# A four-layer transformer kernel on one core: another order of the modulation units in TensorE's stream

## The chip, the core and the metric

The kernel runs on one core of a Trainium2 chip. The core has five engines that run their own instruction streams and meet at semaphores: TensorE (PE, matrix products; its weight loads are listed as PEld), VectorE (DVE), ScalarE (ACT), GpSimd (POOL) and SyncE (SP). SP and ACT issue transfers between HBM and the on-chip memory SBUF; 16 DMA engines carry them. The metric is the device time of one execution in microseconds (us), lower is better. The time of before is the median of three runs.

## What is computed

Two blocks of two layers each work on 256 latent and 256 context tokens with 2048 features in float32. Each layer computes, from a condition vector, shift, scale and gate of its features (the modulation), normalizes and modulates x, projects it, runs attention (in layers 2 and 3 also a multi-scale pooling branch), gates the result to y, projects y and adds it to x by the gate. Cut to the first block:

```python
def first_block(x, c, ctx, c_ctx, w_ada, b_ada, norm_g, w_in, ..., w_out, final_g):
    sc, sc_ctx = jax.nn.silu(c), jax.nn.silu(c_ctx)
    for l in range(DEPTH):
        shift, scale, gate = jnp.split(sc @ w_ada[l] + b_ada[l], 3, axis=-1)
        shift_c, scale_c, gate_c = jnp.split(sc_ctx @ w_ada[l] + b_ada[l], 3, axis=-1)
        h_lat = rms_norm(x, norm_g[l]) * (1.0 + scale[:, None]) + shift[:, None]
        h_ctx = rms_norm(xc, norm_g[l]) * (1.0 + scale_c) + shift_c
        lat_a, lat_b = mixer_inputs(h_lat, w_in[l], ...)
        ctx_a, ctx_b = mixer_inputs(h_ctx, w_in[l], ...)
        o_a, o_b = block_attention(...), block_attention(...)
        x = x + gate[:, None] * merge_groups(o_a, lat_a[3], o_b, lat_b[3], w_out[l])
        ...
    return rms_norm(x, final_g)
```

The modulation `sc @ w_ada[l]` has 2048 x 6144 weights per layer, 48 MB, and depends on the condition alone, so it can be computed at any time before its layer needs it.

## The kernel before

**Slots.** The weights of all projections are 500 slots of 512 KB (`w_raw`, a ring of RAW = 4). Each slot is split into a high part by ACT (`high`, line 589, `w_high`) and a low part by DVE (`low`, line 911, `w_low`), rings of SPL = 2, and PE multiplies three products of high and low parts per block (line 1420, 24 per slot, 512 columns wide where all tokens take part, 256 where only the latent ones do). `low(n)` needs `high(n)`, `high(n)` needs PE to be through with slot n - 2, and SP issues slot n when PE is through with slot n - 4.

**Phases.** `plan_phases` lists them. A layer has: `root` (root of the mean square of x), `apply` (modulation of x into `h_high` and `h_low`, ACT line 647, DVE lines 984 and 1012, one of 16 chunks at a time), then linear phases in rounds of 8 slots k0 to k7: q, kv, cq, ckv, g_mla, kr, g_gqa, short phases and the attention `mla` in layers 0 and 1; q, k, v, pool_v, mix, pool_g, attn_g in layers 2 and 3. Then `ysplit` (ACT line 878 and DVE line 1408 split y from `mix_a` and `mix_b`, called Q and G, into `h_high` and `h_low`) and `out`, four rounds. Layers 0 and 2 work on all tokens, 1 and 3 in most phases on the latent ones. The phases cq to g_gqa (pool_v to pool_g) carry a first attention between their products. (i, k) below is slot k of round i. Round 0 of q and out runs in the order PAIRED, so that its first slots need only the first chunks.

**Units.** The modulation weights are 192 units of 1 MB; 16 of them are a span, the 2048 columns of one of shift, scale and gate of a layer. A unit is four products on PE (`span_unit`, line 1516; the profile counts 8 records). The first 36 run in the opening, from six places: four halves of Q and G, and the two halves of `ada_w`. The other 156 alternate between the two halves of `ada_w`. With `ada = n`, each of a phase's first n rounds has four: two behind slot k1 and two behind slot k5 (`ADA_AFTER = (1, 1, 5, 5)`). The end of a span is followed by a row copy on ACT, four small products on PE (`span_cols`, at k6) and four small adds on DVE (`span_columns`, at the round's end). A span's sum stands in the PSUM bank AD all the while; the attention `mla` uses that bank and B for its outputs in turn.

**SP's queue.** SP issues in the order of the phases, a unit behind the slot behind which it runs. A unit first waits until PE has used the last but one (`ada_used`), since its place is the same. Whatever is behind it in the program waits with it.

**The layer boundary.** After the last products of out, PE sums squares of x by columns (`token_sums`, line 1465), ACT and DVE make the inverse root, PE spreads it (`x_broadcast`, line 1473), DVE and ACT start with `apply`.

**ysplit.** All engines meet at its start (`handed_over`). ACT then issues the load of x from HBM into `x_residual` (lines 869, 872, 875), whose place the attention had used.

## Time and profile before

| | us |
|---|---|
| median of 3 runs | 3137.79 |
| lowest and highest | 3133.08, 3138.83 |
| profiled execution, its own time | 3129.61 |
| its span, first to last instruction | 3127.8 |
| PE busy | 2958.3 (95%) |
| DVE busy | 1587.0 (51%) |
| ACT busy | 1021.5 (33%) |
| mean granted clock of TensorE | 0.977 |

Busy times are those of the profiled execution. A timeline row gives start, length, engine, line, operation, what is written and read, and in brackets the idle time ahead of it with what ended it. "SPq" and "ACTq" are the instructions with which SP and ACT issue a transfer; the length is that of issuing. The granted clock is 1.00 at 2.4 GHz and 0.50 at 1.2 GHz.

### The profile page before, as it was taken

To read this page: it belongs to the slowest core of one execution; us is meant where nothing else is said; L and a number is where in the kernel's file an instruction comes from. 1 tells how busy PE (TensorE), PEld (TensorE's weight loads), DVE (VectorE), ACT (ScalarE), POOL (GpSimd) and SP (SyncE) were. 2 spreads that over 40 slices of the span, in tenths; PEclk is the share of its full clock that TensorE was granted. 3 is DMA by queue.
4 is the path that set the end of the run, shared out by engine and by line. 5 is a ranking of instruction groups with operands and counts; after the bars stand their busy time and mean duration, and the time that the engine had idled before them with its cause. 6 is when DMAs were issued, how large, how long until landed. Compare 5 with 4: busy or idle time off the path is not lost. (4 is left out here: it accounts for less than half of the span.)

```text
span 3127.8 us, 41128 instructions
## 1 busy us (share of the span) xinstructions
PE 2958.3 (95%) x17192; PEld 2372.8 (76%) x17192; DVE 1587.0 (51%) x2512; ACT 1021.5 (33%) x1510; POOL 102.0 (3%) x157
## 2 busy tenths in 40 slices
PE   6899999999998999998999999999989989999988
PEld 2577777776776878886777778767767778798888
DVE  4334434356336544455563553555563365738574
ACT  3222243225113233334332222334441132225453
POOL 0000000000000000000000000430000000004000
PEclk9999999999998999999989999999999989999999
DMA  9644343231544555624745344323455433232455
GB/s 406 267 172 154 126 148 128 88 108 72 186 174 173 204 192 189 221 96 153 279 164 192 129 179 160 136 105 131 155 185 188 172 103 114 93 102 90 146 169 169
DMA packets 129161, 501.94 MB, mean 160 GB/s; under 512 B 14160, under 2 KB 39504, under 8 KB 104144
## 3 DMA queue, kind: packets, MB, share of 16 engines
q1 hardware_dynamic: 109104, 474.96, 42.6%
q10 hardware_dynamic: 19872, 24.35, 2.3%
q8 instruction: 136, 2.23, 0.3%
q14 instruction: 49, 0.40, 0.0%
HBM read 484.05 MB, written 8.39 MB: 157 GB/s over the span
## 5 line engine op out<-in xcount | busy, mean ns | idle before, releaser
L1420 PE MATMUL products<-h_high,w_high 128*128 128x512 f32 (+1 forms) x3424 | 1254.8, 366 | 92.0 <-DVE h_low L1012 30.9
L1420 PE MATMUL products<-h_low,w_high 128*128 128x512 f32 (+1 forms) x3424 | 1194.3, 349 | 0.0
L1420 PE MATMUL products<-h_high,w_low 128*128 128x512 f32 (+1 forms) x3424 | 1193.7, 349 | 0.0
L911 DVE TENSOR_TENSOR w_low<-w_raw,w_high 128x1024 fp32r<-128x1024 f32 x500 | 614.0, 1229 | 807.1 <-ACT w_high L589 803.6
L589 ACT CAST w_high<-w_raw 128x1024 fp32r<-128x1024 f32 x500 | 523.1, 1046 | 1384.8 <-PE products L1420 1243.8
L1420 PEld LDWEIGHTS products<-h_high,w_high 128*128 128x128 f32 x3424 | 662.2, 193 | 298.8 <-issue 151.0
L1420 PEld LDWEIGHTS products<-h_high,w_low 128*128 128x128 f32 x3424 | 662.4, 193 | 81.4
L1420 PEld LDWEIGHTS products<-h_low,w_high 128*128 128x128 f32 x3424 | 664.1, 194 | 78.3 <-issue 10.1
L1420 PE MATMUL products<-w_high,h_high 128*128 128x256 f32 x640 | 183.7, 287 | 5.4 <-DVE w_low L911 4.9
L1420 PE MATMUL products<-w_high,h_low 128*128 128x256 f32 x640 | 181.8, 284 | 0.0
L1420 PE MATMUL products<-w_low,h_high 128*128 128x256 f32 x640 | 181.8, 284 | 0.0
L723 ACT ACTIVATE tmp<-scores,softmax_stats,q_root 128x512 f32<-128x512 f32 (+1 forms) x144 | 101.4, 708 | 173.9 <-DVE softmax_stats L1132 173.9
L1516 PE MATMUL modulation<-ada_w,cond_silu 128*32 128x512 f32 x1264 | 152.3, 599 | 0.0
L1420 PEld LDWEIGHTS products<-w_high,h_high 128*128 128x128 f32 x640 | 123.5, 193 | 13.9 <-DVE w_low L911 7.8
L938 DVE RECIPROCAL tmp<-tmp 128x512 f32<-128x512 f32 (+2 forms) x30 | 118.1, 3938 | 23.7 <-ACT tmp L602 23.7
L1420 PEld LDWEIGHTS products<-w_high,h_low 128*128 128x128 f32 x640 | 123.4, 193 | 0.6 <-issue 0.5
L1420 PEld LDWEIGHTS products<-w_low,h_high 128*128 128x128 f32 x640 | 123.5, 193 | 0.0
L1125 DVE TENSOR_REDUCE softmax_stats<-scores 128x1 f32<-128x512 f32 (+1 forms) x144 | 85.8, 596 | 64.3 <-PE scores L1585 40.6
L710 ACT COPY tmp<-turned 128x512 f32<-128x512 f32 (+1 forms) x96 | 49.3, 513 | 163.6 <-PE turned L1597 163.6
L552 POOL COPY pool_values<-mix_a 128x512 f32<-128x512 f32 (+1 forms) x16 | 11.2, 699 | 2799.2 <-DVE mix_a L1270 2797.8
L1142 DVE RECIPROCAL softmax_stats<-softmax_stats 128x1 f32<-128x1 f32 x192 | 26.5, 159 | 139.7 <-ACT tmp L723 139.0
L647 ACT ACTIVATE h_high<-tmp,ada 128x256 fp32r<-128x256 f32 x128 | 57.5, 501 | 80.6 <-DVE tmp L984 80.6
(217 smaller groups left out, 2610.6 us busy)
## 6 DMA issues: line engine op xcount, KB each, us to landing
w_raw<-w_slots SPq DMA_DIRECT2D x500, 512.0 KB, 3.5
ada_w<-ada_slots SPq DMA_DIRECT2D x168, 1024.0 KB, 7.6
mix_a<-ada_slots SPq DMA_DIRECT2D x12, 1024.0 KB, 14.5
mix_b<-ada_slots SPq DMA_DIRECT2D x12, 1024.0 KB, 15.2
x_scratch<-x_residual ACTq DMA_DIRECT2D x3, 2048.0 KB, 7.8
x_residual<-x_scratch ACTq DMA_DIRECT2D x3, 2048.0 KB, 9.3
x_residual<-x SPq DMA_DIRECT2D x1, 4096.0 KB, 13.4
x_residual<-x ACTq DMA_DIRECT2D x1, 4096.0 KB, 12.9
```

Source lines behind the costliest of these rows:

```text
L552: step(nc.gpsimd.tensor_copy(pool_v[:, seg, PAD:PAD + S], v))
L589: nc.scalar.copy(whi[:, n % SPL, :], raw[:, n % RAW, :]).then_inc(high_done, 1)
L647: last = nc.scalar.activation(hh[:, t, tk], xs(t)[:, tk], ACT.Identity, bias=adaT[:, r, c + st:c + st + 1])
L710: nc.scalar.copy(dst[:, 0:nk], src[:, 0:nk]).then_inc(pt_done, 1)
L723: nc.scalar.activation(tmp[:, t0 + c % ring, 0:nk], src, ACT.Exp, scale=a["scale"] if a["wide"] else q_rs[:, k:k + 1], bias=stat[:, c % 8, ...
L911: nc.vector.tensor_tensor(wlo[:, n % SPL, :], raw[:, n % RAW, :], whi[:, n % SPL, :].bitcast(F32), ALU.subtract).then_inc(low_done, 1)
L938: step(nc.vector.reciprocal(r, r))
L1125: step(nc.vector.reduce_max(stat[:, c % 8, 0:1], src, AX.X))
L1142: step(nc.vector.reciprocal(stat[:, c % 8, 3:4], stat[:, c % 8, 2:3]))
L1420: ins = nc.tensor.matmul(o, a, b, start=first and q == 0, stop=last and q == 2, skip_group_check=skip)
L1516: ins = nc.tensor.matmul(AD[32 * j:32 * j + 32, :], sc32[:, k, :], place[:, j * 512:(j + 1) * 512], start=k == 0, stop=k == KC - 1)
```

## The change

The number of units and their arithmetic stay; their places in the program change.

- Each linear phase now lists its units: `twos` gives the (i, k) behind which a pair runs, `front` how many run ahead of its products. ONE is (0,1), (0,5); SECOND is (1,1), (1,5); FOUR is (0,0), (0,2), (0,4), (0,6); ALONG is ONE, SECOND, (2,1), (2,5), (3,1).
- Before each out phase two units run at the start of `ysplit`, ahead of the engines' meeting. In layers 0 and 1 PE first waits until DVE has read all but the last attention output; the attention's output banks are taken in the other order for that.
- At each of the three layer boundaries six units run: two before the column sums, two behind them, two behind the broadcast. Four of them come from free halves of Q and G (`AWAY`), which SP fills in rounds 2 and 3 of out (`AHEAD`), after y is split; the first two go to `ada_w`, at (3,6) and (3,7).
- Pairs among products, before and after: layer 0: q 4, 4; kv 2, 2; cq 2, 4; ckv 2, 4; g_mla 4, 6; g_gqa 2, 4; out 8, 7. Layer 1: q 4, 1; kv 2, 4; cq 2, 0; ckv 2, 4; g_mla 4, 4; g_gqa 2, 0; out 8, 1. Layer 2: q 4, 1; k 4, 4; v 4, 4; pool_v 4, 4; pool_g 4, 0; attn_g 4, 0; out 8, 7. Layer 3: q 0, 1; out 0, 1.
- A span's columns follow its end at once: `row_copy` and `span_cols` one slot later, `span_columns` two slots later. DVE's wait for the gate columns moves from the start of out to its first evacuation.

```diff
+ONE, SECOND = ((0, 1), (0, 5)), ((1, 1), (1, 5))
+FOUR = ((0, 0), (0, 2), (0, 4), (0, 6))
+ALONG = ONE + SECOND + ((2, 1), (2, 5), (3, 1))
...
-        linear("out", layer, 4, toks, "feat", "res", "X", ada=4 if layer < LAYERS - 1 else 0, ahead=3)
+        linear("out", layer, 4, toks, "feat", "res", "X", front=2,
+               twos=ALONG if layer in (0, 2) else ONE[:1], ahead=3)
...
+        AHEAD = {(2, 3): 2, (2, 7): 3, (3, 2): 4, (3, 4): 5, (3, 6): 0, (3, 7): 1}
...
             def unit(u):
 
                 place, landed, _ = unit_place(u)
-                used = u + 1 - (ADA_RING if u < OPEN_UNITS else 2)
-                if used > 0:
-                    sp.wait_ge(ada_used, used)
+                if UNIT_AT[u][2] is not None:
+                    sp.wait_ge(ada_used, UNIT_AT[u][2] + 1)
+                if u in AWAY:
+
+                    layer = next(ph["layer"] for ph in PH if ph["kind"] == "linear" and u in ph["front"])
+                    sp.wait_ge(y_low, KC * layer)
                 sp.dma_start(place, was[u, :, :]).then_inc(landed, 16)
...
                         for k in range(8):
                             slot(n0 + 8 * i + k)
-                            if ph["name"] == "out" and ph["layer"] < 2 and i == 0 and k == 0:
-
-                                sp.wait_ge(slot_used, n0)
-                            if i < ph["ada"] and k in ADA_AFTER:
-                                for q in range(4):
-                                    if ADA_AFTER[q] == k:
-                                        unit(u0 + 4 * i + q)
+                            if ph["name"] == "out" and (i, k) == (0, 0):
+                                if ph["layer"] < 2:
+
+                                    sp.wait_ge(slot_used, n0)
+                                for u in ph["front"]:
+                                    unit(u)
+                            for u in ph["units"].get((i, k), ()):
+                                unit(u)
+                            if ph["name"] == "out" and ph["layer"] < LAYERS - 1 and (i, k) in AHEAD:
+                                unit(front_of(ph["layer"] + 1)[AHEAD[(i, k)]])
...
-                        if i < ph["ada"] and span_of(at["ada"] + i)[1] == 3:
-                            span_columns(span_of(at["ada"] + i)[0])
+                            for span in columns_at(ph, i, k - 2):
+                                span_columns(span)
...
+                if kind == "ysplit":
+
+                    if ph["layer"] < 2:
+                        pe.wait_ge(o_read, at["att"] - 1)
+                    for u in PH[pi + 1]["front"]:
+                        span_unit(u)
                 handed_over(pi, pe)
...
                     if ph["evac"] == "res" and ph["layer"] < LAYERS - 1:
                         layer, g = ph["layer"], 2 * ph["pairs"] - 1
+                        for u in front_of(layer + 1)[0:2]:
+                            span_unit(u)
 
                         pe.wait_ge(x_summed, at["xsq"] + g)
...
                         token_sums(tmp[:, 1, :], 0, False).then_inc(x_sums, 1)
+                        for u in front_of(layer + 1)[2:4]:
+                            span_unit(u)
                 elif kind == "root":
                     x_broadcast(ph["layer"])
+                    for u in front_of(ph["layer"])[4:6]:
+                        span_unit(u)
```

How the change moves instructions shows best on two engines. First PE at the boundary from layer 0 to layer 1, before: the last products of out, the column sums, the broadcast and the first products of q.

```order
L1420 MATMUL products<-h_high,w_low 128x512
L1465 MATMUL scores<-consts,tmp 128x1 x16
L1473 MATMUL scores<-consts,x_root 128x128 x4
L1420 MATMUL products<-h_high,w_high 128x256
```

And after the change (its lines are numbered otherwise):

```order
L1462 MATMUL products<-h_high,w_low 128x512
L1558 MATMUL modulation<-ada_w,cond_silu 32x512 x8
L1507 MATMUL scores<-consts,tmp 128x1 x16
L1558 MATMUL modulation<-mix_a,cond_silu 32x512 x8
L1515 MATMUL scores<-consts,x_root 128x128 x4
L1558 MATMUL modulation<-mix_b,cond_silu 32x512 x8
L1462 MATMUL products<-h_high,w_high 128x256
```

Three pairs (x8 each) have come in, around the sums and behind the broadcast. Second SP's queue at the start of out in layer 0, before: the slots up to out's k1 (and 24 ahead of it), the pair of (0,1), then k2 to k5, the pair of (0,5), and on.

```order
L463 DMA w_raw<-w_slots 128x1024 [waits slot_used] x26
L486 DMA ada_w<-ada_slots 128x2048 [waits ada_used] x2
L463 DMA w_raw<-w_slots 128x1024 [waits slot_used] x4
L486 DMA ada_w<-ada_slots 128x2048 [waits ada_used] x2
```

And after the change: up to out's k0, the two units of the split, k1, the pair of (0,1), then k2 to k5, the pair of (0,5).

```order
L498 DMA w_raw<-w_slots 128x1024 [waits slot_used] x17
L524 DMA ada_w<-ada_slots 128x2048 [waits ada_used,slot_used]
L524 DMA ada_w<-ada_slots 128x2048 [waits ada_used]
L498 DMA w_raw<-w_slots 128x1024 [waits slot_used]
L524 DMA ada_w<-ada_slots 128x2048 [waits ada_used] x2
L498 DMA w_raw<-w_slots 128x1024 [waits slot_used] x4
L524 DMA ada_w<-ada_slots 128x2048 [waits ada_used] x2
```

Two more units stand ahead of the pair of (0,1), and that pair's wait is now for them, which PE runs at the start of `ysplit`.

## Rows read from the trace of the kernel before

**Rows 1.** The page: busy us of PE; GB/s of 40 slices; the modulation products.
```profile
PE 2958.3 (95%) x17192; PEld 2372.8 (76%) x17192; DVE 1587.0 (51%) x2512; ACT 1021.5 (33%) x1510; POOL 102.0 (3%) x157
...
GB/s 406 267 172 154 126 148 128 88 108 72 186 174 173 204 192 189 221 96 153 279 164 192 129 179 160 136 105 131 155 185 188 172 103 114 93 102 90 146 169 169
...
L1516 PE MATMUL modulation<-ada_w,cond_silu 128*32 128x512 f32 x1264 | 152.3, 599 | 0.0
```

**Rows 2.** Timeline of PE in layer 0's out, round a pair: start, length, instruction.
```profile
778.01 0.39 PE L1420 MATMUL products<-h_high,w_low 128*128 128x512 f32 x1
...
780.19 0.50 PE L1420 MATMUL products<-h_high,w_high 128*128 128x512 f32 x1
```

**Rows 3.** Windows: stretch, length, busy us of the engines, granted clock, DMA share, GB/s.
```profile
971.51:1017.42 45.91, 37.17 (x232) 31.55 (x233) 34.50 (x67) 21.12 (x37) 0.00 (x0) 0.79 0.44 161
2535.08:2579.22 44.14, 34.69 (x200) 31.96 (x201) 34.50 (x67) 21.14 (x37) 0.00 (x0) 0.74 0.26 86
1017.42:1046.79 29.37, 29.11 (x242) 25.80 (x242) 16.81 (x19) 9.58 (x11) 0.00 (x0) 1.00 0.87 301
2579.22:2609.86 30.64, 26.81 (x211) 26.43 (x210) 17.08 (x20) 10.30 (x12) 0.00 (x0) 0.94 0.51 161
...
964.00:984.40 20.40, 12.66 (x52) 11.52 (x53) 14.07 (x34) 9.62 (x19) 0.00 (x0) 0.50 0.39 130
```

**Rows 4.** Timeline: layer 1's out at (1,5), then PE in layer 2's q.
```profile
1519.77 1.92 PE L1516 MATMUL modulation<-ada_w,cond_silu 128*32 128x512 f32 x16
...
1520.30 2.35 DVE L911 TENSOR_TENSOR w_low<-w_raw,w_high 128x1024 fp32r<-128x1024 f32 x2
...
1650.40 0.79 PE L1420 MATMUL products<-h_high,w_high 128*128 128x512 f32 x1 [5.81 <-DVE w_low L911]
```

**Rows 5.** Timeline of PE at the first layer boundary.
```profile
960.14 3.74 PE L1465 MATMUL scores<-consts,tmp 128*128 128x1 f32 x32
966.31 2.08 PE L1473 MATMUL scores<-consts,x_root 128*128 128x128 f32 x8 [2.43 <-DVE x_root L949]
...
971.51 0.55 PE L1420 MATMUL products<-h_high,w_high 128*128 128x256 f32 x1 [3.12 <-DVE h_low L1012]
```

**Rows 6.** Timeline of ACT at the first layer boundary.
```profile
963.86 1.28 ACT L655 ACT_TABLE_LOAD   x1 [1.98 <-issue]
...
965.27 0.19 ACT L657 ACTIVATE x_root<-x_mean_square 128x4 f32<-128x4 f32 x1
```

**Rows 7.** Timeline of PE at the second layer boundary: the broadcast.
```profile
1598.49 2.08 PE L1473 MATMUL scores<-consts,x_root 128*128 128x128 f32 x8 [1.64 <-DVE x_root L949]
```

**Rows 8.** Timeline of SP, ACT and PE: slots for layer 0's out, and its split.
```profile
691.96 1.20 SPq L463 DMA_DIRECT2D w_raw<-w_slots  x2
...
765.30 0.34 ACTq L869 DMA_DIRECT2D x_residual<-x  x1
...
767.27 0.47 PE L1420 MATMUL products<-h_high,w_high 128*128 128x512 f32 x1 [2.45 <-DVE h_low L1408]
```

**Rows 9.** Transfers of the page: issuer, count, size of each, median us to landing.
```profile
x_residual<-x ACTq DMA_DIRECT2D x1, 4096.0 KB, 12.9
```

**Rows 10.** Timeline of ACT and PE at the split of layer 1.
```profile
1462.43 2.88 ACTq L875 DMA_DIRECT2D x_residual<-ctx  x1
...
1466.46 0.55 PE L1420 MATMUL products<-h_high,w_high 128*128 128x256 f32 x1 [5.20 <-DVE h_low L1408]
```

**Rows 11.** DMA queues (q10 ACT's, q1 SP's), 1471.9 to 1476: packets, MB, share.
```profile
q10 hardware_dynamic: 1326, 1.35, 104.2%
q1 hardware_dynamic: 25, 0.10, 6.9%
```

**Rows 12.** The same queues in the opening, 15 to 22 us.
```profile
q1 hardware_dynamic: 320, 2.36, 79.7%
q10 hardware_dynamic: 321, 0.59, 21.9%
```

More of the change, by code:

```diff
@@ L136, in plan_phases @@
             at["fd"] += 1
-            linear("g_gqa", layer, 2, toks, "feat", "gate", "Q", sync=True, ranks="cq", ada=1)
+            linear("g_gqa", layer, 2, toks, "feat", "gate", "Q", sync=True, ranks="cq", twos=(ONE + SECOND, ())[layer])
             def count_ranks():
@@ L407, in quad_bank, with front_of, ends_span, columns_at @@
             return (AD, B)[b % 2]
-        def unit_place(u):
-            if u < OPEN_UNITS:
-                r = u % ADA_RING
-                place = ada_w[:, r - 4, :] if r >= 4 else \
-                    (Q, G)[r // 2][:, 4 * (r % 2):4 * (r % 2) + 4, :].rearrange("p t n -> p (t n)")
-                return place, ada_landed[r], u // ADA_RING + 1
-            return ada_w[:, u % 2, :], ada_landed[4 + u % 2], OPEN_UNITS // ADA_RING + (u - OPEN_UNITS) // 2 + 1
+        UNIT_AT, last_in = [], {}
+        turn = itertools.count()
+        AWAY = {u: r for ph in PH if ph["kind"] == "linear" and len(ph["front"]) == 6
+                for r, u in enumerate(ph["front"][2:])}
+        times = [0] * ADA_RING
+        for u in range(4 * ADA_QUADS):
+            r = u % ADA_RING if u < OPEN_UNITS else AWAY[u] if u in AWAY else 4 + next(turn) % 2
+            times[r] += 1
+            UNIT_AT.append((r, times[r], last_in.get(r)))
+            last_in[r] = u
+        def unit_place(u):
+            r, count, _ = UNIT_AT[u]
+            place = ada_w[:, r - 4, :] if r >= 4 else \
+                (Q, G)[r // 2][:, 4 * (r % 2):4 * (r % 2) + 4, :].rearrange("p t n -> p (t n)")
+            return place, ada_landed[r], count
+        AHEAD = {(2, 3): 2, (2, 7): 3, (3, 2): 4, (3, 4): 5, (3, 6): 0, (3, 7): 1}
+        def front_of(layer):
+            return next(ph["front"] for ph in PH if ph["kind"] == "linear" and ph["name"] == "q" and
+                        ph["layer"] == layer)
+        def ends_span(u):
+            return u >= OPEN_UNITS and u % 4 == 3 and span_of(u // 4)[1] == 3
+        def columns_at(ph, i, k):
+            us = ph["units"].get((i, k), ())
+            return [span_of(u // 4)[0] for u in us if ends_span(u)]
         def split_beside(pi, t, split):
@@ L490, in _ @@
                 if ph["kind"] == "linear":
-                    n0, u0 = at["slot"], 4 * at["ada"]
+                    n0 = at["slot"]
                     def round_(i):
@@ L845, in round_ @@
                             rank_side(ph, 8 * i + k)
[L846 to L849 removed]
+                            for span in columns_at(ph, i, k - 1):
+                                row_copy(ADA_FIRST + span, 4 * (ADA_FIRST + 4 * span) + 16)
                         evac(i, 1)
@@ L1725, in round_ @@
                             rank_side(ph, 8 * i + k)
-                            if beside and k in ADA_AFTER:
-                                for q in range(4):
-                                    if ADA_AFTER[q] == k:
-                                        span_unit(u0 + 4 * i + q)
-                            if beside and k == ADA_COLUMN and span_of(at["ada"] + i)[1] == 3:
-                                span_cols(span_of(at["ada"] + i)[0])
+                            for u in ph["units"].get((i, k), ()):
+                                span_unit(u)
+                            for span in columns_at(ph, i, k - 1):
+                                span_cols(span)
                     rounds(ph, round_)
```

53 lines of the change are left out of this document (28 added, 25 removed).

## The prediction, made before the changed kernel was run

> **What bounds the kernel.** I read the busy table first [rows 1]: TensorE (PE) is busy 95% of 3127.8 us, so outside its gaps whatever is taken out of its stream comes off the end, and 3127.8 - 2958.3 = 169.5 us of gap is all that can be filled. The row of the modulation products there, 152.3 us, is the work that the change reorders. Then timelines of PE: what a pair of units costs among products [rows 2], where a pair already lies in a wait [rows 3, 4], what a layer boundary consists of [rows 5 to 7], and what the splits of y look like with their transfers [rows 8 to 12].
>
> **Price of a pair.** A 512-wide product starts every 0.2265 us. The last before the pair starts at 778.01, the first after it at 780.19 [rows 2]: 780.19 - 778.01 - 0.23 = 1.95 us, and the slot behind a pair runs some 0.17 us longer: 2.12. Where that slot is narrower or carries attention I take 2.05.
>
> **Part 1: pairs among products.** There are 78 before and 65 after; 13 pairs (26 units) leave: 8 units for the four splits of y, 18 for the three boundaries. By layer:
> - Layer 0: +2 in each of cq, ckv, g_mla, +2 in g_gqa, -1 in out. PE has no gap there: 6 x 2.05 + 2 x 2.12 - 2.12 = +14.4.
> - Layer 1: kv +2, ckv +2, cq -2: +4.2 + 4.1 - 4.1 = +4.2. g_gqa -2: -4.1 if nothing waits there, but the ranks' roots on VectorE (DVE) run beside them: I take -3.0. q loses (0,5), (1,1), (1,5). Round 0 of q in layers 1 and 3, with two pairs and with none, takes 45.91 and 44.14 us; round 1, likewise, 29.37 and 30.64 us [rows 3]. So of round 0's two pairs one is free, and that is (0,1), since PE waits for h_low in the slots round it; (0,5) costs 1.8. In round 1 something else waits without pairs, of which layer 1 may have less: -4.1 to 0, I take -3.0. q together -4.8. out loses 7: (0,5) and the three pairs (i,1) give 2.03 each. The pairs (i,5) are over at about 1519.77 + 1.85 = 1521.6, and the w_low of the next slot at about 1520.30 + 1.2 = 1521.5 [rows 4]: without the pair PE waits there, so these three give 0.1 each. A wait of 1.9 us may drop the clock besides (1.4 us each); I take +1.5 for the three. out: -8.4 + 1.5 = -6.9. Layer 1: 4.2 - 3.0 - 4.8 - 6.9 = -10.5.
> - Layer 2: q (0,5) stood before a wait of 5.81 us for w_low [rows 4]: 0; q round 1 -4.2; pool_g and attn_g -8 x 2.05 = -16.4; out -2.1. Layer 2: -22.7.
> - Layer 3: q (0,1) free as above, out (0,1) +2.0.
> Part 1: 14.4 - 10.5 - 22.7 + 2.0 = -16.8, bounds -21 and -11; not 13 x 2.05 = -26.7.
>
> **Part 2: the boundaries.** After the last product come the column sums, the root, the broadcast, and the first h_low. At the first boundary the sums run unbroken from 960.14 for 3.74 us to 963.88, and the broadcast starts at 966.31 [rows 5]. The root starts at 965.27 behind a table load of ScalarE (ACT) that ends at 965.14, not as soon as the sums are there [rows 6]. The first new pair stands ahead of the sums: they end at 963.88 + 1.95 = 965.83, so the root starts near 966.2, 0.95 late. The second pair stands behind the sums, where PE is free only until the broadcast is due at 967.2: it starts at 965.83 + 1.95 = 967.8 at full clock. It took 2.08 us where the granted clock was 0.50 [rows 3], the level of 1.2 GHz, to which it fell after the run of one-column sums; at 2.4 GHz it takes 1.04. So its end moves by +0.5 if the clock holds, and by +3.5 if it is low (the second pair then takes 3.9). At the second boundary PE had 1.64 us before the broadcast [rows 7]: +0.4 or +4.9. The third is as the first. Sum +1.4 to +11.9; nothing shows which level is granted, and I take +6. The third pair stands in the 3.12 us behind the broadcast [rows 5] and, if slow, in the next wait for h_low: nothing. The slots that follow wait for DVE's chain of h_low, which starts at the broadcast, so its delay passes on whole. The next layer's w_slots have 10 us to land: nothing.
>
> **Part 3: spans that follow at once.** Twice in layer 0, (0,2) ends a span and (0,4) begins the next. There PE now waits for DVE's column copies, queued behind the attention's output copy; by the size of such copies some 0.9 each, an estimate: +1.8 (0 to 2.7).
>
> **Part 4: the splits of y.** The pair itself, 1.95 us, fits PE's gaps of 2.45 and 5.20 us [rows 8, 10] and the longer ones of layers 2 and 3. But it frees its halves of ada_w only now. On SyncE's (SP's) queue the next two units wait for that, and w_slots k2 and k3 of out are queued behind them. Before, in layer 0, both slots were issued at 691.96 [rows 8], 75 us early. Now they are issued at about 767, after the units at 765.9 and 766.9, and all behind ACT's load of x_residual (issued 765.30 [rows 8], 12.9 us to land [rows 9]).
> - Layer 0: in line are 4.19 + 2.10 + 0.52 = 6.8 MB; from 766.9 at some 400 GB/s they are through at 783.9: slot landed 784.5, w_high 785.6, w_low 786.8. PE wants it at 780.19: +6.6, and +1.5 if so long a wait drops the clock. If both queues shared evenly the slot would land at 780.6: +2.8. I take +8.1.
> - Layer 1: ACT issues two loads of 2 MB, the second at 1462.43 for 2.88 us [rows 10]; SP's units go at about 1462.3 and 1463.3, the slot at 1463.8. PE wants it ten us after its first product (1466.46), at 1476.9. Of a slot issued at 1471.95 the queue moved 25 packets until 1476.0, while ACT's moved 1326 [rows 11]: the older transfer is drained first. By that the slot lands near 1480: +5.5. If the units get through first: 0. I take +4.
> - Layer 2: the slot is wanted 14 us after the first product: 0. Layer 3: only w_slot k3 falls behind ACT's load: 0 to 2, I take +1.
> - A fuller gap may keep the clock at 2.4 GHz in layers 1 and 3, where at 1.2 GHz the first slot loses 24 x 0.12 = 2.9 us: up to -5, I take -1.
> Part 4: 8.1 + 4 + 1 - 1 = +12, bounds +1 and +19.
>
> A rule bears on layer 1. The trace has 25 packets against 1326 there. The Trainium skill, "DMA: Bandwidth & Descriptors", section "Queues, rings and completion order", says that an engine serves its queue rows in turn, a packet at a time. In the opening this trace agrees: 320 packets of one queue beside 321 of the other [rows 12]; at the split it doesn't. By the rule the 8 KB packets of the units get most of the time beside ACT's of 1 KB, layer 1 costs 0, and the sum below is -1 instead of +3.
>
> **Sum.** -16.8 + 6 + 1.8 + 12 = +3. The profiled execution took 3129.61 us (span 3127.8, 1.8 around it); the median of the three runs is 3137.79, 8.2 more. On its own execution the sum gives 3132.6; the change is what I forecast, so it goes on the median: 3140.8.
>
> **Rivals.**
> - **The gaps are filled for nothing (faster).** The weights land in time at the splits and the clock holds at the boundaries: -16.8 + 1.4 + 1.8 + 3 = -11, 3127. For it: gaps of 2.4 us and more are there, and in the opening two queues share. Against it: rows 11.
> - **SP's queue and a low clock (slower).** SP blocks w_slots k2 and k3 at the splits of layers 0 and 1, 8 and 7 us, and the second pair runs at 1.2 GHz at all boundaries: -16.8 + 11.9 + 1.8 + 17 = +14, 3152. It decides once parts 2 and 4 together pass 21.3 us; I have them at 18.
> - **Every pair is worth its price (much faster).** 26.7 off: 3111. Against it: rows 3 and 4, where pairs already lay in waits, and rows 5, where the pair ahead of the sums has no gap.
> - **Denser pairs starve the products.** A round with 8 units moves 8.4 + 4.2 = 12.6 MB in at least 8 x 5.44 + 4 x 2.05 = 51.7 us, 244 GB/s, where the opening reached 406 [rows 1]: unlikely, and +5 at most, inside the range.
>
> **Chances.** 0.2% (6.3 us) is about what a measurement of this kernel can tell from no change. No change (3131.5 to 3144.1) 0.42; slower 0.32; faster 0.26, of which 0.05 for the full gain. The range leaves out the full gain and the far end of the slower case: 3122 to 3157. The likeliest case's own is 3131 to 3147.
>
> **What will show it.** Right, if in layer 0's out the slot k2, which began 780.19 - 767.27 = 12.9 us after the first product, begins about 7 us later, with ACT's w_high waiting for a transfer; if the broadcast ends 0.5 to 5 us later after the last product than the 966.31 + 2.08 - 960.3 = 8.1 us of before; if PE waits 1.9 us for w_low at k6 of layer 1's out rounds. Wrong, if no w_high waits for a transfer at the splits (the time then falls by 8 us or more), or if the clock stays low long after the new waits (it then passes 3150).

## The result, and the profile after the change

The changed kernel takes 3146.75 us (median of 13 runs, 3140.55 to 3153.3), the kernel before, in 13 runs beside it, 3137.34 us. The ratio is 1.0032, 95% interval 1.0023 to 1.0041: some 10 us slower, small but measured. The forecast was 3140.8 and "no change"; what came lies in its range, in the case that had 0.32.

The profiled execution of the changed kernel took 3146.80 us, 17.2 more than that of before (3129.61), where the medians differ by 9.4: before's profiled execution was 7.7 us faster than its own median. That gap has to be kept apart from the change; the last section shows what such gaps can consist of.

The page of the changed kernel, with the busy times, the largest group of products with its idle time, and two kinds of transfers. Busy PE rose by 3.9 us against [rows 1] (2958.3), so some 13 of the 17 us are idle time. The last column of the transfers is the time from issue to landing:

```profile
PE 2962.2 (94%) x17192; PEld 2372.6 (75%) x17192; DVE 1586.2 (50%) x2512; ACT 1022.0 (32%) x1510; POOL 101.7 (3%) x157
...
L1462 PE MATMUL products<-h_high,w_high 128*128 128x512 f32 (+1 forms) x3424 | 1255.8, 367 | 107.8 <-DVE w_low L950 49.1
...
x_residual<-x_scratch ACTq DMA_DIRECT2D x3, 2048.0 KB, 17.8
x_residual<-x ACTq DMA_DIRECT2D x1, 4096.0 KB, 14.6
```

**Layer 0's split**, timeline of ACT, SP and PE (start, length, instruction, idle time ahead of it). It answers to [rows 8]:

```profile
782.41 1.92 PE L1558 MATMUL modulation<-ada_w,cond_silu 128*32 128x512 f32 x16 [0.26 <-issue]
784.61 0.47 PE L1462 MATMUL products<-h_high,w_high 128*128 128x512 f32 x1 [0.28 <-DVE h_low L1450]
...
797.87 1.93 PE L1558 MATMUL modulation<-ada_w,cond_silu 128*32 128x512 f32 x8 [2.13 <-DMA ada_w<-ada_slots]
800.36 1.94 PE L1558 MATMUL modulation<-ada_w,cond_silu 128*32 128x512 f32 x8 [0.56 <-DMA ada_w<-ada_slots]
803.98 0.80 PE L1462 MATMUL products<-h_high,w_high 128*128 128x512 f32 x1 [1.68 <-DVE w_low L950]
...
783.52 1.19 SPq L524 DMA_DIRECT2D ada_w<-ada_slots  x2
784.75 11.34 SPq L498 DMA_DIRECT2D w_raw<-w_slots  x4
...
801.62 1.04 ACT L630 CAST w_high<-w_raw 128x1024 fp32r<-128x1024 f32 x1 [13.39 <-DMA w_raw<-w_slots]
```

The pair of the split does lie in the old gap: 782.41, and the first product follows at 784.61. The bill comes with the next pair, (0,1). Its two units were issued from 783.52 and arrive one after the other, 2.13 and 0.56 us late. Each half of that pair took 1.93 us, where the whole pair at the start of the fence takes 1.92: the clock had fallen. Then comes the 1.68 us for k2's w_low. Slot k2 began 803.98 - 784.61 = 19.4 us after the first product, against 12.9 before.

**Layer 1's split**, timeline of ACT, PE and DVE, answers to [rows 10]:

```profile
1481.96 0.60 ACTq L911 DMA_DIRECT2D x_residual<-x_scratch  x1
1482.59 6.63 ACTq L914 DMA_DIRECT2D x_residual<-ctx  x1
...
1490.37 0.55 PE L1462 MATMUL products<-h_high,w_high 128*128 128x256 f32 x1 [6.76 <-DVE h_low L1450]
...
1509.47 2.36 DVE L950 TENSOR_TENSOR w_low<-w_raw,w_high 128x1024 fp32r<-128x1024 f32 x2 [7.76 <-DMA x_residual<-ctx]
...
1510.76 0.58 PE L1462 MATMUL products<-h_high,w_high 128*128 128x256 f32 x1 [4.99 <-DVE w_low L950]
```

Two things stand here that the prediction didn't have. ACT needs 6.63 us to issue the load of ctx (2.88 before, [rows 10]), and the h_high behind it on ACT, with the first product, come that much later: 1490.37 - 1481.96 = 8.4 us after the first load's issue, 1466.46 - 1461.80 = 4.7 before. And PE waits for no w_slot: ACT waits 2.46 us for one, k2's, but its w_low is ready when PE gets there. DVE waits 7.76 us for x itself, ahead of w_low of k4, and PE behind it 4.99 us. The two loads of x, times from issue to landing, after and (second fence) before:

```profile
DMA to landing us min/median/max: 17.8/22.3/26.9
```

```profile
DMA to landing us min/median/max: 9.3/13.2/17.1
```

The longer time is that of ctx, the second load.

**Layer 2's split** has the first of the two as well. ACT's issue of ctx there, after and (second fence) before:

```profile
2331.72 6.18 ACTq L914 DMA_DIRECT2D x_residual<-ctx  x1
```

```profile
2325.07 2.55 ACTq L875 DMA_DIRECT2D x_residual<-ctx  x1
```

**The first boundary** after the change, timeline of PE; it answers to [rows 5]:

```profile
983.76 1.92 PE L1558 MATMUL modulation<-ada_w,cond_silu 128*32 128x512 f32 x16
985.61 4.05 PE L1507 MATMUL scores<-consts,tmp 128*128 128x1 f32 x32
989.59 3.23 PE L1558 MATMUL modulation<-mix_a,cond_silu 128*32 128x512 f32 x16
993.09 1.15 PE L1515 MATMUL scores<-consts,x_root 128*128 128x128 f32 x8 [0.27 <-issue]
994.17 1.93 PE L1558 MATMUL modulation<-mix_b,cond_silu 128*32 128x512 f32 x16
997.36 0.36 PE L1462 MATMUL products<-h_high,w_high 128*128 128x256 f32 x1 [1.27 <-DVE h_low L1051]
```

The last product ends at 983.8, the broadcast at 994.24: 10.4 us, against 8.1. The pair behind the sums took 3.23 us, most of it at the low clock, and the broadcast behind it only 1.15 (2.08 before). The window of that pair (stretch, length, busy times, granted clock, DMA share, GB/s):

```profile
989.59:992.82 3.23, 3.23 (x17) 0.58 (x16) 0.83 (x5) 0.20 (x1) 0.00 (x0) 0.58 0.99 381
```

By stage, from the first product of each phase to the next, after minus before in the two profiled executions: layer 0 ahead of its split +17.3 (of it -2.2 beside the opening, where kernels with the same instructions differ by up to 3 us); out's round 0 there +8.3; its round 3 and the boundary, with one pair less, +0.2; layer 1's phases up to g_gqa -5.7, its split +3.75, out's round 0 +4.8 (with one pair less), rounds 1 to 3 and the second boundary -4.0; layer 2's q to mix -1.1, pool_g and attn_g with the split -13.3 (of it -0.7 in attn_g's last round with the split), out and the third boundary +0.5; layer 3 +2.4 until out, +4.0 in out's round 0. The sum is +17.2.

### The profile page after: what moved, and what is told of

Read it like the earlier page. It is cut to its first block and busy times, and to the rows that moved or that the text cites. A ratio compares the mean times of both kernels' runs of the same rounds, so it can differ in the third digit from the quotient of the medians.

```text
span 3145.0 us, 41144 instructions
## 1 busy us (share of the span) xinstructions
PE 2962.2 (94%) x17192; PEld 2372.6 (75%) x17192; DVE 1586.2 (50%) x2512; ACT 1022.0 (32%) x1510; POOL 101.7 (3%) x157
## 5 line engine op out<-in xcount | busy, mean ns | idle before, releaser
L1558 PE MATMUL modulation<-ada_w,cond_silu 128*32 128x512 f32 x1168 | 142.4, 605 | 5.0 <-DMA ada_w<-ada_slots 2.7
```

The lines of the kernel that those rows point to most:

```text
L1558: ins = nc.tensor.matmul(AD[32 * j:32 * j + 32, :], sc32[:, k, :], place[:, j * 512:(j + 1) * 512], start=k == 0, stop=k == KC - 1)
```

## Experiments

"Against the changed kernel" below is the difference of two ratios to the kernel before, times 3137 us; at five rounds it is known to some 4 us. Stages are compared in the profiled executions, between the first products of phases.

### 1. What holds the splits up

> The changed kernel, but at the start of each out SP issues the w_slots k2 and k3 ahead of the pair of units of (0,1), which waits for the place of the units that run at the split. Theory 1 (as predicted: w_slots are held up in SP's queue behind those units and drained behind ACT's load of x): the w_high of k2 in layer 0 no longer waits (13.4 us of idle ACT in the changed kernel), layer 0's out loses its 8.3 us, layer 1's 4.8, layer 3's 1.5: about -14 us. Theory 2 (the units of (0,1) are themselves late, since their transfers share the DMA engines with the load of x): TensorE still waits 2.1 + 0.6 us for ada_w in layer 0 and runs the pair at half clock, only the 1.7 us of w_low and the half-clock slot behind it go: -3.5 us there, nothing in layer 1, -1 in layer 3: about -4 us.

```diff
                         for k in range(8):
-                            slot(n0 + 8 * i + k)
+                            early = ph["name"] == "out" and i == 0
+                            if not (early and k in (2, 3)):
+                                slot(n0 + 8 * i + k)
+                            if early and k == 1:
+                                slot(n0 + 2)
+                                slot(n0 + 3)
```

Measured: 3134.54 us, ratio 0.9997 (0.9988 to 1.0006), 11 us less than the changed kernel. Timeline of PE, layer 0, and of DVE, layer 1:

```profile
800.01 1.07 PE L1563 MATMUL modulation<-ada_w,cond_silu 128*32 128x512 f32 x8 [2.46 <-DMA ada_w<-ada_slots]
802.49 1.91 PE L1563 MATMUL modulation<-ada_w,cond_silu 128*32 128x512 f32 x8 [1.42 <-DMA ada_w<-ada_slots]
```

```profile
1503.38 2.56 DVE L955 TENSOR_TENSOR w_low<-w_raw,w_high 128x1024 fp32r<-128x1024 f32 x2 [3.89 <-DMA x_residual<-ctx]
```

In layer 0 the w_slots are early, and the wait for them is gone, but the units still come 2.46 and 1.42 us late; out's round 0 falls by 2.55 us, not by 8.3. So most of layer 0's loss stays as the units' own lateness, by theory 2; part of that lateness, 3.88 us of waits instead of 2.69, is the 1 MB of w_slots now ahead of them. Layer 1 falls by 5.3 us, which theory 2 had at 0: 1 MB of w_slots was carried before the split, and ctx lands after 23.1 us instead of 26.9, so that DVE waits 3.89 us, not 7.76. Neither theory was right there; both counted only the transfer that each had in mind.

> The changed kernel, but VectorE's wait for the loads of x stands before its first evacuation of out, not at the phase's start ahead of w_low of k4. Theory 1 (late w_slots): no change, 0 us. Theory 2 (in layer 1 the two loads of x land 9.8 us later than before because the units share the engines, and w_low of k4 is queued behind VectorE's wait for them): the wait of 4.99 us before k4 of layer 1's out goes, with some 1.5 to 2 us of half clock behind it, -5 to -7 us there; nothing in layers 0, 2 and 3.

```diff
-                    if ph["evac"] == "res":
-                        dve.wait_ge(x_in, X_IN[layer])
...
                             if g == 0:
+                                dve.wait_ge(x_in, X_IN[layer])
                                 dve.wait_ge(ada_ready, columns_ready(layer, 3))
```

Measured: 3140.39 us, ratio 1.0009 (1.0000 to 1.0018), 7 us less. Layer 1's out, round 0, falls by 6.8 us. The late data of layer 1 is x's, not a w_slot's, and the place of the wait for it, ahead of work that doesn't need it, is what makes it cost.

> The changed kernel, but the first pair of out runs behind k4 in layers 0, 1 and 2 and behind k3 in layer 3 instead of behind k1 (and layer 0's and 2's next two pairs at (0,7) and (1,2)), so that SP issues it only once TensorE is through with k0 and no w_slot of the start is behind it. Theory 1 (queue): layer 0 -8.3, layer 1 -4.8, layer 3 -1.5, while the late start of layer 1's split stays (+3.75): -14 us. Theory 2 (shared engines): the same, and ACT's issue of the load of ctx, 6.63 us beside the units' transfers, is back at 2.9 us, so that layer 1's first product comes 3.75 us earlier too: -18 us. If the units inside the splits were themselves dear, less than half of either would come back.

```diff
-ALONG = ONE + SECOND + ((2, 1), (2, 5), (3, 1))
+ALONG = ((0, 4), (0, 7), (1, 2), (1, 5), (2, 1), (2, 5), (3, 1))
...
-               twos=ALONG if layer in (0, 2) else ONE[:1], ahead=3)
+               twos=ALONG if layer in (0, 2) else ((0, 4 if layer == 1 else 3),), ahead=3)
```

Measured: 3135.30 us, ratio 0.9991 (0.9982 to 1.0000), 13 us less. Layer 0's out -8.45, layer 1's split -3.78, layer 2's split -3.4: as expected, and ACT's issue of ctx is back at 2.85 us in layer 1. But layer 1's out got 4.1 slower and layer 3's 5.6. Timeline of ACT, DVE and PE in layer 1, and of DVE in layer 3:

```profile
1490.78 1.05 ACT L630 CAST w_high<-w_raw 128x1024 fp32r<-128x1024 f32 x1 [1.95 <-DMA w_raw<-w_slots]
...
1499.28 2.36 DVE L950 TENSOR_TENSOR w_low<-w_raw,w_high 128x1024 fp32r<-128x1024 f32 x2 [9.08 <-ACT w_high L630]
...
1500.56 0.58 PE L1462 MATMUL products<-h_high,w_high 128*128 128x256 f32 x1 [8.34 <-DVE w_low L950]
```

```profile
3038.48 2.36 DVE L950 TENSOR_TENSOR w_low<-w_raw,w_high 128x1024 fp32r<-128x1024 f32 x2 [8.80 <-DMA x_residual<-x_scratch]
```

In both layers it is x again. In layer 3 the row names it. In layer 1 the profile puts DVE's wait down to ACT, whose w_high of k5 ends at 1499.28; but the first of DVE's two instructions is w_low of k4, whose w_high was there at 1491.83, and ctx, issued at 1474.97, landed 24.3 us later, at 1499.27. The pair's units, issued at 1483.98, now share the engines with a later part of the same load. The wait had only moved.

> The changed kernel with what the first runs showed put right at the splits: w_slots k2 and k3 of out ahead of the units in SP's queue, out's first pair behind k4 in layers 0 and 2 (the next two at (0,7) and (1,2)), layer 1's only pair behind (1,5), where TensorE waits for w_low anyway, and VectorE's wait for x before its first evacuation. If the units' transfers beside the loads of x are the cause: layer 0's out -8.4, ACT's issue of ctx back at 2.9 us in layers 1 and 2 (-3.8 and -3.4), layer 1's out -9 (wait 5.0, pair 1.9, half clock 1.7), layer 3 -1.2: -26 us, 3121. If only the queue order counts, as predicted: -14 us, 3133.

The edit is those of the first two kernels, ALONG as in the third, and for the single pair:

```diff
-               twos=ALONG if layer in (0, 2) else ONE[:1], ahead=3)
+               twos=ALONG if layer in (0, 2) else ((1, 5) if layer == 1 else (0, 1),), ahead=3)
```

Measured: 3121.78 us, ratio 0.9952 (0.9940 to 0.9964), 25 us less than the changed kernel and 0.5% faster than before. By stage: layer 0's out -8.5, layer 1's split -3.7 and out's round 0 -7.1, layer 2's split -3.4, layer 3's out -3.3. This puts a number on the splits: all but 1 to 2 us are theirs, some 23 us (known to some 4). The rest is the pair now at (1,5), which lies for 1.3 us in a wait of PE (1.74 us without it, 0.41 with it).

### 2. How two queues share the DMA engines

> The changed kernel, but ACT issues layer 0's load of x as four transfers of 1 MB, whose rows in SBUF are 8 KB long, as the units' are, not one of 4 MB with rows of 32 KB. If the 16 DMA engines take a packet of each queue in turn (39 packets of ACT's queue beside 34 of SP's from 787 to 791 us in the changed kernel, but 1.28 MB beside 0.28), the units get half of the bandwidth instead of a fifth: both have landed near 796.5 instead of 800.2, TensorE's waits for ada_w of 2.1 and 0.6 us go, and w_slot k2 lands some 2 us earlier: -3 to -5 us in layer 0's out. If the older transfer is drained first (as I had read from before's rows), nothing changes: 0.

```diff
-                        act.dma_start(xT[:, :, :], dram["x0"]).then_inc(x_in, 16)
+                        for c in range(4):
+                            act.dma_start(xT[:, 4 * c:4 * c + 4, :], dram["x0"][:, 4 * c:4 * c + 4, :]
+                                          ).then_inc(x_in, 16)
```

Measured: 3147.95 us, ratio 1.0040 (1.0028 to 1.0052): no gain. But the sharing came out as the first theory says. DMA queues from 787 to 795 us (queue: packets, MB, share of the engines' time; q10 is ACT's, q1 SP's), in the changed kernel and then with x in pieces:

```profile
q10 hardware_dynamic: 86, 2.82, 81.5%
q1 hardware_dynamic: 80, 0.66, 19.7%
```

```profile
q1 hardware_dynamic: 222, 1.69, 50.3%
q10 hardware_dynamic: 225, 1.70, 50.1%
```

Packets are as many in both queues in each kernel; bytes are not. With packets of 32 KB against 8 KB, x got 2.82 of 3.48 MB; with rows of 8 KB it got half. Layer 1 shows the other side. The changed kernel from 1487 to 1491 us, where ACT's packets have 1 KB and the units' 8 KB:

```profile
q1 hardware_dynamic: 193, 1.45, 87.5%
q10 hardware_dynamic: 198, 0.20, 15.1%
```

Again a packet each, and here x gets an eighth of the bytes (a fifth from 1490 to 1495 us, where most of SP's packets are the 4 KB ones of w_slots: 341 beside 344): it lands 26.9 us after its issue (17.1 before), and that is the wait of DVE. The rule of the Trainium skill ("DMA: Bandwidth & Descriptors", "Queues, rings and completion order"), which I had put aside, is what both kernels do.

With x in pieces the waits for ada_w are gone (one unbroken pair at 798.62), and PE waits instead for k2's w_slot, which is in line with the same bytes. Timeline of PE and ACT:

```profile
782.19 2.10 ACTq L909 DMA_DIRECT2D x_residual<-x  x4
...
804.62 0.79 PE L1464 MATMUL products<-h_high,w_high 128*128 128x512 f32 x1 [4.07 <-DVE w_low L952]
```

4.07 us in one wait for the 4.37 in three, and 1.8 us more for ACT's four issues ahead of its h_high. I had expected the slot 2 us earlier; it wasn't, since a fairer share changes who waits, not when the 6.8 MB are through.

What, then, did [rows 11] show? Before, a slot issued at 1471.95 had 25 packets moved by 1476, ACT's queue 1326. Two other windows of the kernel before, 1471.9 to 1475.3, and 1461.8 to 1475.3, from the issue of the loads of x on:

```profile
q10 hardware_dynamic: 1153, 1.18, 109.8%
```

```profile
q10 hardware_dynamic: 3914, 3.99, 93.2%
```

The slot's first packet moved 3.4 us after its issue, and by then ACT's two loads, 4096 packets of 1 KB, were all but through. So the window on which I rested the order of drainage can't tell an order from a delay: it is mostly the time before the first packet. The changed kernel can. There the units were issued at 1482.80, their first packet moved at 1485.97, with over 3400 of ACT's 4096 still to come, and from then on the two queues took turns, as the window above shows.

### 3. The boundaries

> The changed kernel without units at the layer boundaries: q of layers 1 to 3 has four pairs among its products, at (0,1), (0,5), (1,1), (1,5), as q had in layers 1 and 2 before. Theory 1 (the boundaries cost about 2.3 us each, and of q's pairs one or two lie in waits): boundaries -7, layer 1's q +1 and +4, layer 2's q -2.6 and +4.2, layer 3's q +1.8 and -1.3: about 0. Theory 2 (nine units' pairs in the boundaries were free, each pair among products costs 2.05): +18 us. Theory 3 (the boundaries cost the far end of their bounds, 11.9): -5 us.

```diff
-        q_units = dict(twos=((0, 1), (0, 5)) + SECOND) if layer == 0 else dict(front=6, twos=ONE[:1])
+        q_units = dict(twos=ONE + SECOND)
```

Measured: 3157.51 us, ratio 1.0066 (1.0053 to 1.0078), 11 us more than the changed kernel. The stages with the boundaries fall by 2.3, 1.0 and 2.2 us; q costs 0 and +4.3 in layer 1, -2.0 and +4.2 in layer 2, +2.7 and +3.7 in layer 3, where I had +1.8 and -1.3. The total lies between the first theory's 0 and the second's 18. So the boundaries are a good place for units, and the sizes of the first theory hold but for layer 3's q.

> The changed kernel, but at each layer boundary no pair runs ahead of the column sums: the first one stands behind them, the second and third behind the broadcast. Theory 1 (the pair ahead of the sums costs 0.95 us of the root and pushes the second into the broadcast, 2.3 us a boundary together): the broadcast ends 1 to 2 us earlier after out's last product, the two pairs behind it (3.9 us) fit the 3.1 us wait for h_low with 0.8 us over: -1 us each, -3 us. Theory 2 (TensorE's clock falls behind the one-column sums and doubles the pair behind them): 0.

```diff
                     if ph["evac"] == "res" and ph["layer"] < LAYERS - 1:
                         layer, g = ph["layer"], 2 * ph["pairs"] - 1
-                        for u in front_of(layer + 1)[0:2]:
-                            span_unit(u)
...
-                        for u in front_of(layer + 1)[2:4]:
+                        for u in front_of(layer + 1)[0:2]:
...
-                    for u in front_of(ph["layer"])[4:6]:
+                    for u in front_of(ph["layer"])[2:6]:
```

Measured: 3144.98 us, ratio 1.0030 (1.0018 to 1.0042): -1 us, not to be told from 0 or from -3. Timeline of PE at the first boundary:

```profile
987.75 4.89 PE L1507 MATMUL scores<-consts,tmp 128*128 128x1 f32 x32
992.58 3.64 PE L1558 MATMUL modulation<-ada_w,cond_silu 128*32 128x512 f32 x16
996.47 1.36 PE L1515 MATMUL scores<-consts,x_root 128*128 128x128 f32 x8 [0.25 <-issue]
```

The sums now start 1.9 us earlier, but they themselves take 4.89 us instead of 4.05, and the pair 3.64 instead of 3.23, the whole of it at 1.2 GHz:

```profile
992.58:996.22 3.64, 3.64 (x17) 0.59 (x16) 0.83 (x5) 0.49 (x3) 0.00 (x0) 0.50 1.04 348
```

The broadcast ends 10.08 us after the sums' start, which was 8.63 us in the changed kernel with the pair of 1.85 us ahead of it: 0.4 us gained of the 1 to 2 expected. By stage the three boundaries with the first round of q come to -1.2, -3.3 and -0.4 us. This experiment doesn't decide between its theories; it bounds the order within a boundary to a few us.

### 4. The issue of ctx on ACT's queue

Five kernels carry the same edit: ACT issues ctx behind its first four h_high.

```diff
-                        if layer < 3:
-
-                            act.dma_start(xT[:, :, 0:S], dram["ctx2"]).then_inc(x_in, 16)
...
                         split_beside(pi, t, high)
+                        if t == 3 and 0 < layer < 3:
+                            act.dma_start(xT[:, :, 0:S], dram["ctx2"]).then_inc(x_in, 16)
```

> As the kernel with cleared splits, but in layers 1 and 2 ACT issues the load of ctx behind its first four h_high, not ahead of them. If issuing it (2.9 us) holds up the split of y: the first product of out comes 2.9 us earlier in layer 1 and some 2 us in layer 2, -5 us against the kernel with cleared splits. If something else starts the split's products (w_high of k1, which then stands behind the issue), the gain is given back there: 0. If ctx lands too late for the first evacuation: slower by 1 to 5 us.

Measured: 3113.31 us, ratio 0.9926 (0.9914 to 0.9938), 8 us less than with cleared splits alone. Layer 1's split -2.8, layer 2's -2.8, as expected; the largest of the rest are -3.1 and -4.5 us in the rounds with the first two boundaries, where nothing was edited; such rounds differ by up to 3 us and more between kernels with the same instructions there, by the time at the low clock. PE in layer 1, where the pair of the split and the first product now follow one another:

```profile
1474.18 1.92 PE L1560 MATMUL modulation<-ada_w,cond_silu 128*32 128x512 f32 x16 [0.26 <-issue]
1476.38 0.36 PE L1464 MATMUL products<-h_high,w_high 128*128 128x256 f32 x1 [0.28 <-DVE h_low L1452]
```

> As the kernel with cleared splits and ctx behind h_high, and at the boundaries the column sums first, as in the kernel with sums first. If the boundary's own order is worth 1 to 1.6 us each: 3 to 5 us less than without it, 3109. If the pair behind the sums runs at half clock and gives it back: 0, 3113.

Measured: 3112.29 us, ratio 0.9918 (0.9904 to 0.9931), the fastest of all, but within the error of the one before it. It beats before by 0.8% and the changed kernel by 1.1%.

> The kernel before, with one edit: in layers 1 and 2 ACT issues the load of ctx behind its first four h_high. If the 2.9 and 2.6 us of issuing stand on the path to out's first product: -2.8 us each, -5.6 us. If a wait behind it takes the gain (w_high of k1, or VectorE's wait for ctx, which then lands about 3 us later): 0.

Measured: 3145.05 us, ratio 1.0029 (1.0018 to 1.0040): 9 us slower than before, where I had expected -5.6 or 0. Layer 1's split does fall by 2.9 us, and layer 2's by 2.6; but in layer 1's out, DVE and PE:

```profile
1490.93 2.36 DVE L910 TENSOR_TENSOR w_low<-w_raw,w_high 128x1024 fp32r<-128x1024 f32 x2 [13.42 <-DMA x_residual<-ctx]
```

```profile
1492.21 0.58 PE L1419 MATMUL products<-h_high,w_high 128*128 128x256 f32 x1 [10.64 <-DVE w_low L910]
```

ctx, issued some 3 us later, lands 25.5 us after its issue instead of 17.1, because w_slots of 4 KB packets and then a pair's units of 8 KB take their turns beside its 1 KB ones (from 1480 to 1485 us 235 packets of SP's, 1.78 MB, beside 242 of ACT's, 0.25 MB). The kernel before stood close to this edge: its ctx landed at 1462.43 + 17.1 = 1479.5, and w_low of k4 was due at 1481.3.

> The changed kernel with that same edit alone: ctx behind the first four h_high, the units beside it as they are. In both layers the first product of out comes some 6.5 us earlier, since ACT no longer stands 6.6 and 6.2 us at issuing. If the engines' bandwidth sets when ctx has landed, VectorE's wait for it before w_low of k4 ends as late as now in layer 1, and TensorE's wait before k4 grows by what was gained: layer 1 0, layer 2, which has no such wait, -5 to -6: -6 us in all. If issuing was the cause by itself: -12 us.

Measured: 3141.47 us, ratio 1.0014 (1.0004 to 1.0023), 6 us less than the changed kernel. The split falls by 6.5 us in layer 1 and 6.2 in layer 2; layer 1's out, round 0, gives 3.5 back and its round 1 3.0 more. The 3.0 are the clock's: that round lasts 27.2 us in the traces of the changed kernel and of the one with x in pieces, 28.7 in the one with slots first, and 30.2 to 30.5 in this and three others with the same instructions there. So bandwidth takes back about half of layer 1's gain, and layer 2 keeps its own. Timeline of PE in layer 1:

```profile
1498.38 1.93 PE L1557 MATMUL modulation<-ada_w,cond_silu 128*32 128x512 f32 x8 [2.71 <-DMA ada_w<-ada_slots]
```

What PE waits for is no longer x alone (2.42 us before k4) but also the units of (0,1) (0.79 and 2.71 us) and w_low of k2 (2.08 us), whose w_slot is late: the products now start before the transfers are there.

> The kernel before with both edits: ctx behind the first four h_high, and VectorE's wait for x at its first evacuation of out. If VectorE's wait ahead of w_low of k4 alone made the first of these edits slower (it took 10.6 us of TensorE's time in layer 1's out): that wait is gone, ctx (25.5 us to land) meets the first evacuation about 2 us late, and the kernel is 3 to 6 us faster than before, 3131 to 3134. If w_slots are late there for the transfers' sake as well: no better than before, 3137 to 3141. Set against the kernel with cleared splits and ctx behind h_high (3113.3), which has both edits too, it gives the worth of the change's other order of units once the splits are cleared: about 18 us.

The edit is the one above and that of the second kernel. Measured: 3133.83 us, ratio 0.9990 (0.9981 to 0.9999), 3 us faster than before, at the near end of what was expected. DVE's wait for x is gone, and layer 1's out has another in its place: ACT now stands for 10 us at issuing a load of 256 KB behind ctx (0.34 us in the kernel before, 1.58 with the first of the two edits alone, 5.60 with cleared splits and ctx behind). Timeline of ACT and PE:

```profile
1472.41 10.12 ACTq L880 DMA_DIRECT2D rope_heads<-rope_diff  x1
```

```profile
1485.30 0.58 PE L1420 MATMUL products<-h_high,w_high 128*128 128x256 f32 x1 [5.29 <-DVE w_low L910]
```

Against this kernel, the one with cleared splits and the same two edits (3113.31) is 20 us faster. So the change's order of units is worth up to 20 us once nothing at the splits stands in its way; up to, because this kernel's 10 us of issuing, and PE's wait of 5.29 us behind it, are in the difference.

## Where the prediction failed, and where it held

The sum was +3, measured were +9.4 by the medians. Two parts erred in opposite directions, and that the time still lies in the range is partly luck: the splits cost some 10 us more than forecast, by a cause that no rival named, and the rest of the change gained 3 us more.

- **Part 4, the splits of y, was the step that failed: +12 forecast (bounds +1 to +19), some +23 measured.** In layer 0 the size was right (+8.1 forecast, +8.3 measured) and so was the sign to look for (w_high waiting 13.39 us for a transfer), but the reason was half of it: of the 8.3 us, 2.7 are waits for the units themselves, which I had let run in time, 1.7 the wait for w_low, and the rest the clock, on which I had put 1.5. In layer 1, +4 forecast and some +10.5 measured (3.75 in the split, 4.8 in out's round 0, and the 2.0 of a pair that had left that round), by the stages of the two traces, where all four layers together come to 24. The named mechanism, a late w_slot k3, didn't occur. What occurred was not among the rivals: the load of x became the late transfer, by the wait of DVE ahead of w_low and by ACT's 6.63 us of issuing. In layer 2, 0 forecast; ACT's issue there took 3.6 us more. Layer 3: +1 beside the pair forecast, +1.9 measured.
- **The rule that I put aside was right.** I rejected the sharing by turns on [rows 11], a window of 4.1 us in which the slot's first packet hadn't moved for the first 3.4, and ACT's queue was nearly empty when it did. By the rule layer 1's w_slots come in time, which they did as far as PE is concerned. But the 0 us that I drew from it for layer 1 was wrong too: if the units get more, x gets less, and I priced one of the two sides. Both of my readings asked only when the weights land.
- **The rest of the change did better than forecast.** With the splits' 25 us taken out (cleared splits against the changed kernel, one hidden pair of 2.0 included), it gains 15 us. The terms that answer to it are -16.8 + 6 + 1.8 - 1 - 2.0 = -12. The 3 us between are less than the error of either.
- **Price of a pair: held.** cq, ckv and g_mla in layer 0 took 5.0, 4.2 and 5.9 us more for two more pairs each (2 x 2.05 forecast), cq and g_mla with a wait of 0.8 us for a span that follows at once (0.9 estimated), g_mla with one more span's columns besides (0.96 us, which stood elsewhere before). The count was two off: 80 pairs stood among products before and 67 after, not 78 and 65, since q's first round in layer 0 runs four of the 36 units that the text gives to the opening (1264 + 16 records of line 1516 are 160 units). The difference of 13, on which the sum rests, is right.
- **Pairs in waits: held in layer 1's out, not in the numbers of q.** PE waits 1.74 us for w_low at k6 of rounds 1 to 3 there, as forecast (1.9), and the clock fell behind that wait in two of three rounds of the changed kernel's trace, in none of the last two in the one with slots first. q: layer 1 -5.1 (-4.8 forecast), layer 2 -1.6 (-4.2), since its first round rose by 2.6 behind the boundary. For layer 3 I had used the difference of two layers of unlike work, and the kernel without boundary units showed +3.7 for q's round 1, where that difference said -1.3.
- **Boundaries: held.** +2.3 us of delay of the first broadcast, within the 0.5 to 5 forecast, three times some 2 us, +6 forecast for all. Which clock the second pair gets was open, and the trace shows the low one for most of it.
- **Layer 2's pool_g and attn_g: -13.3 instead of -16.4.** The difference is ACT's issue of ctx again.

The nearest rival was "SP's queue and a low clock (slower)", 3152. The time went its way, about half as far, by another mechanism.

## What to carry to other kernels

When work with transfers is moved into a gap that a barrier leaves, list every transfer in flight there, with bytes, packet size and who waits for it in which order, the old ones too: here the moved one arrived late, and it also made a load late that had until then been just in time. A wait belongs ahead of the first use and not at the head of a phase, and an engine that splits weights shouldn't issue long transfers ahead of that. Before a share is read from a window of a queue's packets, find the first packet of the transfer in question, and see how much the other queue has left. And where the profile puts a wait down to one engine, check the time at which each of the things waited for was there: one wait for x looked like a wait for a weight.

## What the runs showed of the hardware that I had not expected

- **Bytes go by the size of packets.** Two queues with work move a packet each: 86 beside 80 (32 and 8 KB), 225 beside 222 (8 and 8 KB), 198 beside 193 (1 and 8 KB). In bytes that is 2.82 beside 0.66 MB, 1.70 beside 1.69 and 0.20 beside 1.45.
- **A transfer behind a full queue of another engine starts late.** The first packet moved 1.4 us after the issue when nothing was under way (ACT's load at 1461.80 in the kernel before), and 3.2 to 3.9 us after it when ACT's queue was full (SP's at 1482.80 after, 1471.95 before, 1469.36 in the kernel before with two edits).
- **Issuing a transfer can hold an engine for long.** With 2 MB of 1 KB packets ahead in its queue ACT needed 2.88 us for the next issue; beside the units' transfers 6.63. One and the same load of 256 KB behind 4 MB took 0.34, 1.58, 3.49, 5.60 and 10.12 us to issue in five kernels, so it isn't the load's own shape. Whether ACT waits for its own queue or for something that it shares with SP's issuing isn't shown. How many packets a queue takes before that, these runs don't settle either: 430 had moved when the issue of 2.88 us ended, 936 at the one of 6.63.
- **The clock is chance in part.** Two executions of the same stretch of the same instructions, layer 1's out round 2 in the changed kernel and in the one with slots first, and layer 2's mix before and in the kernel with two edits, which changes nothing there (windows: stretch, length, busy times, granted clock, DMA share, GB/s):

```profile
1552.16:1582.76 30.60, 26.52 (x194) 26.11 (x193) 17.21 (x18) 9.97 (x12) 0.00 (x0) 0.89 0.56 209
```

```profile
1545.91:1573.55 27.64, 23.55 (x195) 23.14 (x193) 17.20 (x18) 9.97 (x12) 0.00 (x0) 1.00 0.64 229
```

```profile
2066.86:2088.45 21.59, 18.69 (x56) 8.58 (x55) 12.76 (x22) 3.61 (x7) 11.06 (x16) 1.00 0.37 147
```

```profile
2068.99:2093.61 24.62, 21.71 (x56) 9.58 (x55) 12.76 (x22) 3.60 (x7) 11.05 (x16) 0.86 0.33 127
```

3 us each time, at 1.2 GHz behind a wait of some 2 us or not at all. A few such steps would be enough for the 11 us between the fastest and the slowest execution of the kernel before, and for the 7.7 us by which before's profiled execution lay under its median: behind layer 1, the kernel with two edits is slower than it in mix by 3.0, in attn_g by 1.6 and in layer 3's k by 1.6 us, with no edit there, and faster in layer 2's v by 1.2. How much of the 7.7 us is the clock's isn't shown: of 70 executions of the kernel before, the ten with a mean granted clock of 0.973 took 3138.2 us on average, the three with 0.977 3134.2. What decides whether the clock falls at a given wait, no run here tells.
